# Expert results added to their tokens by TensorE instead of through a buffer in DRAM

## What is computed

```python
x = x + hierarchical_moe(rmsnorm(x, norm2_g), ...)
return rmsnorm(x, final_g)

def hierarchical_moe(h, ...):
    ...                                  # group, top 2 experts of it, their weights
    def expert_block(args):
        e, rows_tok, rows_w = args
        xb = tok[rows_tok]
        a = xb @ w_gate[e]               # 1024 x 512
        u = xb @ w_up[e]                 # 1024 x 512
        y = (jax.nn.silu(a) * u) @ w_down[e]     # 512 x 1024
        return (y * rows_w[:, None]).astype(tok.dtype)
    ...
    out = jnp.zeros((T, D), tok.dtype).at[row_tok].add(ys.reshape(n_rows, D))
```

## Time and profile before

| | |
|---|---|
| median of 3 runs | 1699.04 us (1697.4 to 1700.35) |
| the profiled execution, its time | 1699.08 us |
| the profiled execution, its span in the trace | 1697.2 us |
| TensorE busy | 1477.6 us (87%), in the last quarter less |
| VectorE, ScalarE, GpSimd busy | 34%, 28%, 29% |
| DMA engines, from 1200 us to 1594 us | busy all the time, 424 GB/s |
| indirect DMAs, issue to landing | gathers 14.1 us, scatters 10.4 us (median) |

### The profile page before, as it was taken

How to read it: one execution, slowest core, us unless ns; L and a number is a source line. 1 busy time by engine, 2 the same in 40 slices (tenths; PEclk the granted TensorE clock), 3 DMA queues, 4 the chain that set the end, 5 groups by cost and what they waited for, 6 DMA issues and landing times.

```text
span 1697.2 us, 18562 instructions
## 1 busy us (share of the span) xinstructions
PE 1477.6 (87%) x7132; PEld 979.0 (58%) x7133; DVE 585.2 (34%) x964; ACT 475.4 (28%) x818; POOL 487.8 (29%) x286
## 2 busy tenths in 40 slices
PE   7999999999699999999995999993977778787792
PEld 5975667887588888788684675573322233222230
DVE  3146654213633333321418695745100000000003
ACT  4245564222433333221424324221100000000001
POOL 3531134444334444444332373422001000010000
PEclk9999999999899999999997999996999998999996
DMA  7323002232223332223222221167899999999894
GB/s 287 109 88 86 1 2 63 90 97 88 86 87 99 99 100 91 96 89 97 87 87 88 81 75 52 48 245 293 327 428 427 426 429 427 425 423 422 358 384 192
DMA packets 48263, 317.33 MB, mean 187 GB/s; under 512 B 7696, under 2 KB 7696, under 8 KB 35776
## 3 DMA queue, kind: packets, MB, share of 16 engines
q1 hardware_dynamic: 40240, 295.13, 45.5%
q0 software_dynamic: 7376, 19.13, 3.1%
q10 hardware_dynamic: 576, 2.10, 0.3%
HBM read 308.00 MB, written 14.68 MB: 190 GB/s over the span
## 4 chain that ended last, share of the span: by engine, by line
PE 64%; DMA 19%; DVE 9%; issue 3%; ACT 2%; POOL 1%; SPq 0%; POOLq 0%; DVEq 0%; ACTq 0%
PE banks L357 24%; DMA arena<-experts 17%; PE banks L387 11%; PE banks L981 8%; PE banks L1961 3%; PE banks L868 2%; PE banks L367 2%; PE banks L1003 2%; PE banks L1890 2%; PE banks L1906 2%; DMA rows<-arena 1%; PE banks L725 1%; PE banks L1873 1%; PE banks L726 1%; PE banks L1877 1%
## 5 line engine op out<-in xcount | busy, mean ns | idle before, releaser
L335 POOL TENSOR_TENSOR arena_r<-ring,arena_r 128x1024 fp32r<-128x1024 f32 x143 | 354.0, 2477 | 503.5 <-ACT arena_r L320 503.5
L357 PE MATMUL banks<-hT_r,arena_r 128*128 128x512 f32 x1216 | 391.8, 392 | 8.5 <-DVE arena_r L1738 5.4
L320 ACT ACTIVATE arena_r<-ring 128x1024 fp32r<-128x1024 f32 x143 | 151.3, 1059 | 517.0 <-PE banks L357 318.2
L357 PE MATMUL banks<-arena_r 128*128 128x512 f32 x800 | 293.4, 392 | 0.0
L981 PE MATMUL banks<-ring,arena 128*64 128x512 f32 x720 | 228.1, 622 | 59.0 <-DMA arena<-experts 40.4
L357 PEld LDWEIGHTS banks<-hT_r,arena_r 128*128 128x128 f32 x1216 | 228.7, 188 | 67.0 <-issue 9.3
L387 PE MATMUL banks<-arena_r 128*128 128x512 f32 x784 | 187.5, 393 | 3.6 <-POOL arena_r L335 3.6
L981 PEld LDWEIGHTS banks<-ring,arena 128*64 128x64 f32 x720 | 75.0, 143 | 200.1 <-issue 149.0
L387 PEld LDWEIGHTS banks<-arena_r 128*128 128x128 f32 x784 | 147.2, 188 | 38.3 <-POOL arena_r L335 5.3
L357 PEld LDWEIGHTS banks<-arena_r 128*128 128x128 f32 x800 | 150.5, 188 | 32.3
L605 POOL DMA_INDIRECT back<-arena,at_out x16 | 16.1, 1007 | 430.9 <-DVE arena L1479 216.5
(11 more groups left out here) (421 smaller groups left out, 1812.3 us busy)
## 6 DMA issues: line engine op xcount, KB each, us to landing
arena<-experts SPq DMA_DIRECT2D x49, 2048.0 KB, 19.0
ring<-experts SPq DMA_DIRECT2D x45, 2048.0 KB, 18.3
ring<-stream SPq DMA_DIRECT2D x163, 512.0 KB, 3.5
rows<-arena POOLq DMA_DIRECT2D x8, 512.0 KB, 7.1
arena<-back SPq DMA_DIRECT2D x8, 512.0 KB, 7.1
grow<-grows POOLq DMA_DIRECT2D x5, 512.0 KB, 4.5
resid<-x ACTq DMA_DIRECT2D x4, 512.0 KB, 5.3
hT<-experts SPq DMA_DIRECT2D x1, 2048.0 KB, 19.1
```

Of the source, the lines that this page charges most:

```text
L320: nc.scalar.activation(parts(name, m)[:, 0, :], tile(tile_n), ACT.Copy).then_inc(S["w_high"], 1)
L335: nc.gpsimd.tensor_tensor(w[:, 1, :], tile(tile_n), plain(w[:, 0, :]), ALU.subtract).then_inc(S["w_low"], 1)
L357: last = nc.tensor.matmul(pb[:, bank, :], w[:, a, k * P:(k + 1) * P], b[:, k, :], start=(k == 0 and part == 0), stop=(k == ND - 1 and part ...
```

## The change

The store of `rows` is made once (four DMAs), and the index of a slot is the token. The buffers `back`, `G`, `ysb` and `xo` are gone, with the scatters and the loads of `back`.

In their place the router also makes `p_of`, the weight of each slot (eight more tensor_scalars of 128 x 128 and eight more matmuls), and keeps the token of each slot in f32 (`token_of`). For each pair VectorE forms `spread_r`, a 0/1 matrix of 128 slots x 512 tokens (one comparison). The down product of 128 slots x 1024 is taken out of PSUM times the slot's weight, in two parts whose sum is f32: ScalarE writes `y_high`, rounded to fp32r (twice 128 x 512), and VectorE `y_low`, the rest (twice 128 x 512, each behind the ScalarE part). `place` then multiplies: for each of four blocks of 128 tokens four matmuls of 128 x 512 in fp32r (two halves of the width, high and low), and VectorE adds the two banks to `X` (`add_pair`, 128 x 1024). `place` of pair b - 1 stands between the gate and the up product of pair b, and uses banks 3, 4 and 5, 6 in turn; the third and fourth block wait for the add that frees their banks. That of pair 15 stands behind it, with all eight banks.

`Xg` is cleared by GpSimd before each gather from pair 2 on. The three chunks loaded ahead are now chunk 0 of pair 4, chunk 1 of pair 8 and chunk 2 of pair 12; the third is issued when the first two gathers have landed. The pair loops are written out on all engines. The norm's squares on ScalarE wait for the last adds directly, the final scaling is made in place in `X`, and the branch to the overflow passes stands behind the last adds on VectorE. Unused constants are dropped.

```diff
-        rows = nc.dram_tensor("rows", (2 * T, D), F32).ap()
-        back = nc.dram_tensor("back", (2 * T, D), F32).ap()
+        at_tok, at_p = sb("at_tok", [P, 1]), sb("at_p", [P, 1])
+        rows = nc.dram_tensor("rows", (T, D), F32).ap()
...
-        ysb = ar3(24576, 2, D)
+        y_high, y_low = [ar_r(off, D) for off in (24576, 25600)]
...
+        token_of, p_of = ar(27136, P), colt[:, 512:512 + P]
+        spread_r = colt_r[:, 0:T]
+        token_row = cs("alibi")
+        STEADY, LAST = [(3, 4), (5, 6), (3, 4), (5, 6)], [(0, 1), (2, 3), (4, 5), (6, 7)]
...
-        SPARE = (N_PAIR - 2, [[(hT[:, :, :].rearrange("p k t -> p (k t)"), 0, CHUNK)], [(ar(0, CHUNK), 0, CHUNK)],
-                              [(ar(4096, 1536), 0, 1536), (ar(6656, 1536), 1536, 3072), (junk[:, :], 3072, CHUNK)]])
...
+        SPARE = {0: 4, 1: 8, 2: 12}
...
-            for j in range(2 * NT):
-                pool.dma_start(rows[j * P:(j + 1) * P, :], xn[:, j % NT, :]).then_inc(S["rows_st"], 16)
+            for i in range(NT):
+                pool.dma_start(rows[i * P:(i + 1) * P, :], xn[:, i, :]).then_inc(S["rows_st"], 16)
...
+            def cleared(b, q):
+                pool.wait_ge(S["x_tr"], b * 2 + 2)
+                pool.sem_inc(S["gathers"], 1)
+                nc.gpsimd.memset(Xg[:, q, :], 0.0).then_inc(S["xg_zero"], 1)
+                pool.wait_ge(S["xg_zero"], b)
+            for b in range(N_PAIR):
+                if b >= 2:
+                    cleared(b, b % 2)
+                gather(b, b % 2, idx[:, BLOCKS * b:BLOCKS * b + 1])
...
+                    sp.dma_start(place, EX[6 * SPARE[c] + c, :, first:end]).then_inc(S["spare_in"], 16)
             sp.wait_ge(S["w_used"], W_EXP)
             spare_in(0)
-            sp.wait_ge(S["rows_st"], 16 * 2 * NT)
+            sp.wait_ge(S["rows_st"], 16 * NT)
             spare_in(1)
             sp.wait_ge(S["counts_out"], 1)
+            sp.wait_ge(S["xg_in0"], 16)
+            sp.wait_ge(S["xg_in1"], 16)
             spare_in(2)
-            with sp.Fori(1, SPARE[0]) as b:
+            for b in range(1, N_PAIR):
                 for c in range(6):
-                    sp.wait_ge(done[c // 2], b)
-                    sp.dma_start(chunk(c), EX[b * 6 + c, :, :]).then_inc(chunk_in[c], 16)
-            for b in range(SPARE[0], N_PAIR):
-                for c in range(3 if b == SPARE[0] else 0, 6):
-                    sp.wait_ge(done[c // 2], b - 1 if c < 3 and b > SPARE[0] else b)
-                    sp.dma_start(chunk(c), EX[b * 6 + c, :, :]).then_inc(chunk_in[c], 16)
+                    if not spared(b, c):
+                        sp.wait_ge(done[c // 2], b - 1 if spared(b - 1, c) else b)
+                        sp.dma_start(chunk(c), EX[b * 6 + c, :, :]).then_inc(chunk_in[c], 16)
...
-            sp.wait_ge(S["fin_go"], 1)
-            for i in range(NT):
-                for c in range(2):
-                    sp.dma_start(G[:, 2 * i + c, :], back[(NT * c + i) * P:(NT * c + i + 1) * P, :]).then_inc(S[f"back{i}"], 16)
             for i in range(NT):
                 sp.wait_ge(S["fin_y"], i + 1)
-                sp.dma_start(out[i * P:(i + 1) * P, :], xo[:, i, :]).then_inc(S["out_st"], 16)
+                sp.dma_start(out[i * P:(i + 1) * P, :], X[:, i, :]).then_inc(S["out_st"], 16)
...
+            for j in range(2 * NT):
+                pe.wait_ge(S["slot_ready"], 2 * NT + j + 1)
+                last = nc.tensor.matmul(pb[:, 2, 0:P], slot_row[:, j, :], slot_value[:, j, :], start=(j == 0), stop=(j == 2 * NT - 1))
+            last.then_inc(S["rank_mm"], 1)
...
+                if not isinstance(b, int) or b >= 1:
+                    pe.wait_ge(S["y_lo"], b * 2)
+                    pe.wait_ge(S["added"], b * NT if not isinstance(b, int) else b * NT - 1)
+                both_in(b, 4)
...
+            def place(b, banks):
+                pe.wait_ge(S["spread"], b + 1)
+                pe.wait_ge(S["y_hi"], b * 2 + 2)
+                pe.wait_ge(S["y_lo"], b * 2 + 2)
+                for i in range(NT):
+                    if banks is STEADY and not (isinstance(b, int) and b == 0 and i < 2):
+                        pe.wait_ge(S["added"], b * NT + max(i - 1, 0))
+                    elif banks is LAST and i == 0:
+                        pe.wait_ge(S["added"], b * NT)
+                    for h in range(2):
+                        for part, y in enumerate((y_high, y_low)):
+                            last = nc.tensor.matmul(pb[:, banks[i][h], :], spread_r[:, i * P:(i + 1) * P], y[:, h * 512:(h + 1) * 512],
+                                                    start=(part == 0), stop=(part == 1))
+                    last.then_inc(S["placed"], 1)
+            def pair_pe(b, half, q):
                 turn_rows(b, half, q)
                 pe.wait_ge(S["x_ev_dve"], b + 2)
                 pe.wait_ge(S["x_ev_act"], b + 2)
-                product(b, 0, 0, S["ex_gate"], skipped)
-                product(b, 2, 1, S["ex_up"], skipped)
+                product(b, 0, 0, S["ex_gate"])
+                if isinstance(b, int) and b >= 1:
+                    place(b - 1, STEADY)
+                product(b, 2, 1, S["ex_up"])
                 turn_hidden(b)
-                down(b, skipped)
+                down(b)
             pe.wait_ge(S["counts_out"], 1)
-            with pe.Fori(0, SPARE[0] // 2) as turn:
-                for q in range(2):
-                    pair_pe(turn * 2 + q, turn, q)
-            for q in range(2):
-                pair_pe(SPARE[0] + q, SPARE[0] // 2, q, q > 0)
+            for b in range(N_PAIR):
+                pair_pe(b, b // 2, b % 2)
+            place(N_PAIR - 1, LAST)
...
-            for q in range(2):
-                pair_act(q, 0, q)
-            with act.Fori(1, N_PAIR // 2) as turn:
-                for q in range(2):
-                    pair_act(turn * 2 + q, turn, q)
+                for h in range(2):
+                    nc.scalar.activation(y_high[:, h * 512:(h + 1) * 512], pb[:, 3 + h, :], ACT.Copy, scale=p).then_inc(S["y_hi"], 1)
+            act.wait_ge(S["p_ready"], 1)
+            for b in range(N_PAIR):
+                pair_act(b, p_of[:, BLOCKS * b:BLOCKS * b + 1])
+            for i in range(NT):
+                act.wait_ge(S["added"], NT * (N_PAIR - 1) + i + 1)
+                square(act, "n5", i, X[:, i, :])
+                root(act, "n5", i)
...
+            for j in range(2 * NT):
+                TS(slot_value[:, j, :], cs("iota"), column[:, j:j + 1], RT[:, 880 + j:881 + j], ALU.is_equal, ALU.mult)\
+                    .then_inc(S["slot_ready"], 1)
+            for i in range(NT):
+                L(TS(token_row[:, i * P:(i + 1) * P], cs("iota"), float(P * i), None, ALU.add))
             counts = RT[0:1, 1400:1432]
             nc.vector.tensor_copy(counts, pb[0:1, 0, 0:32]).then_inc(S["counts_out"], 1)
-            def pair_rows(b, half, q):
+            dve.wait_ge(S["rank_mm"], 3)
+            nc.vector.tensor_copy(p_of, pb[:, 2, 0:P]).then_inc(S["p_ready"], 1)
...
+            def spread_rows(tokens):
+                TS(spread_r, token_row, tokens, None, ALU.is_equal).then_inc(S["spread"], 1)
+            def pair_hidden(b, p):
                 dve.wait_ge(S["ex_up"], b + 1)
                 dve.wait_ge(S["ex_sig"], b + 1)
                 TT(hb, sil, pb[:, 1, :], ALU.mult).then_inc(S["ex_hid"], 1)
-                dve.wait_ge(S["ex_down"], b + 1)
-                if not opening(b):
-                    dve.wait_ge(S[f"y_st{q}"], half * 16)
-                nc.vector.tensor_copy(ysb[:, q, 512:1024], pb[:, 4, :]).then_inc(S["y_ev_dve"], 1)
-            pair_rows(0, 0, 0)
+                for h in range(2):
+                    dve.wait_ge(S["y_hi"], b * 2 + h + 1)
+                    STT(out=y_low[:, h * 512:(h + 1) * 512], in0=pb[:, 3 + h, :], scalar=p, in1=plain(y_high[:, h * 512:(h + 1) * 512]),
+                        op0=ALU.mult, op1=ALU.subtract).then_inc(S["y_lo"], 1)
+            def add_pair(b, banks):
+                for i in range(NT):
+                    dve.wait_ge(S["placed"], b * NT + i + 1)
+                    if not (isinstance(b, int) and b == 0):
+                        dve.wait_ge(S["added"], b * NT + i - (NT - 1))
+                    first, second = banks[i]
+                    TT(X[:, i, :], X[:, i, :], pb[:, first:second + 1, :].rearrange("p b c -> p (b c)"), ALU.add).then_inc(S["added"], 1)
...
+            for b in range(N_PAIR):
+                if b:
+                    pair_rows(b)
+                    add_pair(b - 1, STEADY)
+                spread_rows(token_of[:, BLOCKS * b:BLOCKS * b + 1])
+                pair_hidden(b, p_of[:, BLOCKS * b:BLOCKS * b + 1])
+                if b == 0:
+                    dve.wait_ge(S["over_ready"], 1)
+                    some = dve.value_load(over[0:1, 0:1], min_val=0, max_val=1)
+            add_pair(N_PAIR - 1, LAST)
...
-            for i in range(NT):
-                dve.wait_ge(S[f"back{i}"], 32)
```

(6 more changed lines are left out.)

163 lines of the change are left out of this document (64 added, 99 removed).

## The result

The changed kernel takes 1703.82 us (median of 8 runs, 1702.47 to 1710.01), the kernel before, beside it, 1699.01 (8 runs, 1696.73 to 1700.35). The ratio is 1.0035, with a 95% interval of 1.0023 to 1.0047: **slower** by 4.8 us, or 0.35%. The profiled execution took 1703.4 us, with a span of 1701.5, against 1697.2 before.

| stretch | before | after | difference | forecast |
|---|---|---|---|---|
| to the first add behind the last dense product (L1363, now L1360) | 1137.36 | 1148.94 | +11.6 | 0 |
| from there to the eviction of pair 0 | 79.0 | 68.9 | -10.1 | -7.5 |
| eviction of pair 0 to that of pair 15 | 451.1 | 465.85 | +14.7 | +11.9 |
| eviction of pair 15 to the end | 29.7 | 17.8 | -12.0 | -12.0 |

The account below looks back on a forecast made before the run. Loads bound the expert part before; the change was to move the bound to TensorE's chain. Span 1697.2 + 10.9 + 1.0 - 7.5 - 12.0 = 1689.6, with 1.88 us around it 1691.5 us; range 1676 to 1705.

Parts of the forecast that it names:

- The one nearest in time, at 1704.5: Rival: the start gives nothing and place takes 5.2 us; 1704.5 us, chance 0.09.
- The loads to TensorE: Expert pairs: the bound moves from the loads, 29.3 us a pair, to TensorE; DMA share 0.95 to 0.98.
- The chain: TensorE's work per expert pair: 25.0 + 4.6 + 1.2 = 30.8 us; +10.9 us over fifteen pairs.
- The eviction: Between pairs: the gate product starts 2.94 us after the eviction's start instead of 1.62; 1.2 us more a pair.
- The register load: VectorE's load of a register ahead of pair 1: 1.0 us more (0 to 2).
- The clock: Rival: longer waits in the pairs make TensorE's granted clock fall, 1.7 us each; ten falls give 1708.5 us; chance 0.17.
- The start: Before pair 0: half the stores and one chunk less ahead let the first gather land earlier; -7.5 us.
- The third chunk's hold: In the start: holding this chunk until both gathers are in leaves 2.1 MB less ahead of the gather, 5 us.
- The tail: From the last eviction to the end: 17.7 us instead of 29.7, -12.0 us.
- the branch behind them: In the tail: VectorE's branch behind the last add takes 1.0 us (0 to 2.5).

Follow-up runs that it names:

- e1: Changed kernel with the old list of constants, so the arena stands at its old address: 1691.49 us, ratio 0.9964 to the kernel before.
- e2: Kernel before with the changed kernel's list of constants and nothing else of the change: 1711.84 us, ratio 1.0075.
- x1: On e1, VectorE copies the turned rows before making the low parts, and the gate product waits for ScalarE's copy only at its fifth step: 1665.92 us.
- e9: On e1, place multiplies only the high parts, 8 matmuls a pair instead of 16: 1677.72 us.
- e14: On e1, the third early chunk is issued once the counts are out, without waiting for the first two gathers: 1691.43 us.
- e10: On e1, the tokens are stored in DRAM twice, as before the change (eight stores): 1702.96 us.
- e3: Changed kernel with an empty 64-byte buffer between the constants and what follows, arena 128 bytes off a multiple of 256 from hT: 1698.4 us.
- e6: On e1, an empty 64-byte buffer at the very start moves every buffer by 64 bytes and keeps all distances: 1692.67 us.
- x2: On x1, TensorE also turns the next pair's rows behind the up product, while VectorE makes the hidden product: 1660.28 us, ratio 0.9774.
- x3: On x2, the dense down product's rows stand 32 columns lower, at a multiple of 256 bytes from the weights: 1658.21 us.

## Why the prediction was wrong

The value, 1691.5, lay 12.3 us under the measured one, inside the range. The direction, faster with a chance of 0.68, was wrong.

**The step that failed** is one that the sum does not even show as a term: it starts from the old span, 1697.2, and adds only what happens behind the router, taking what stands ahead of it as it was. The term for the stages ahead of the router was put at nothing without a reason. The change speaks against that in one place, the shorter `CSTS` ("unused constants are dropped"), which shifts the arena by 448 bytes. In the up stage it changed the pitch of the fp32r matmuls from 226.2 to 233.9 ns, which is 7.3 us between 492 and 705 us, and with other stages it came to 11.6 us by the last dense product. e1 and e2 show that this list by itself is worth 12.3 and 13.0 us, in either kernel. With it the prediction's own terms give 1703.1, and the changed kernel takes 1703.8.

None of the rivals was this. The one nearest in time, at 1704.5, was made of other things: a start that is 4 us later than forecast (one that gives nothing, as it is called, would be 7.5 later), where it came 2.6 us sooner, and place at 5.2 us, where it took 4.8. That the value lies inside the range is luck: the range was not made for this term.

**The loads to TensorE.** Right. The DMA share fell to 0.96, between the 0.95 and 0.98 that were named, and the waits for loads are gone.

**The chain.** Forecast 30.8 us a pair, measured 30.93 (29.8 to 31.5 were allowed). Place takes from the gate's last matmul to the up's first 1325.43 - 1320.66 = 4.8 us, forecast 4.6, and the adds hold it as described: the third group starts 2.50 us after the first, forecast 2.39.

```profile
1320.66 2.11 PE L996 MATMUL banks<-arena_r,colt_r 128*128 128x512 f32 x8
...
1323.16 2.34 PE L996 MATMUL banks<-arena_r,colt_r 128*128 128x512 f32 x8 [0.39 <-DVE resid L1495]
```

The eviction, too: ScalarE starts at 1310.86, and the gate product at 1313.64, 2.78 us later, forecast 2.94.

```profile
1313.64 0.64 PE L956 MATMUL banks<-hT,arena 128*64 128x512 f32 x1 [1.81 <-DVE arena L1473]
```

The size was right, but the prediction took this wait as the price of the change. x1 shows that most of it was the price of one order: the two low parts are not needed until place, 7 us later, and stood ahead of the copy on which TensorE waits. (x1 also lets the gate product start without ScalarE's copy; the two edits were not run apart.)

**The register load**, 1.0 us ahead of pair 1: the first pair is 31.12 us against 30.93, so 0.2.

**The clock.** The rival with a chance of 0.17 happened in small. One pair of the changed kernel took 32.61 us at a granted clock of 0.95, in the gate product behind the ordinary wait of 1.8 us, which took 8.8 us there instead of 7.0. e1 had two such pairs, e9 four, the other runs with this wait one to three, and x1, whose wait is 0.35 us, none. The row of that product on the timeline:

```profile
1530.17 8.78 PE L956 MATMUL banks<-ring,arena 128*64 128x512 f32 x32 [1.80 <-DVE arena L1473]
```

A fall costs 1.7 us, as the prediction took from the earlier trace rows; ten falls were far too many. The Trainium skill (TensorE: Matmul & The Clock Gate, A second HAM failure mode: psum-queue depth-cycling) would have them come from short waits between groups of matmuls; in the changed kernel the fall stands behind the long wait after the transposes, not behind the short ones inside place, and x1, which keeps the short ones and shortens the long one, has none. The falls may also explain part of the spread of the changed kernel's eight runs, though only one of them was profiled: the slowest, 1710.01 us, has the lowest mean clock (0.971) and the fastest, 1702.47, the highest (0.976).

**The start.** Forecast -7.5, measured -10.6 in e1 (1216.35 to 1205.70) and -10.1 in the changed kernel. The time of the row transposes was right: 1179.99 us in e1, forecast 1181. The way there was not. The stores were not done at 1172 but before 1162.45, when the chunk that waits for them was issued; the four stores, issued from 1154.34 on, were done within 8.1 us, where eight took 20.4 from the last one's issue. So the index alone set the gather. The third chunk's hold, to which 5 us were put down, gains nothing (e14). And 2.3 us came from TensorE, which no longer idles for 9 us (e10; 14 in the kernel before) and is at the full clock sooner; the sum had no term for that.

**The tail.** Forecast 17.7 us, measured 17.8. The first add ends 4.8 us behind the eviction's start, forecast 4.6. All four are done after 9.2 us, forecast 8.1, since the second and the third wait for their matmuls; but the branch behind them, forecast at 1.0, costs nothing, and so the scalings start where they should. VectorE's adds and its last scaling:

```profile
1687.34 1.22 DVE L1495 TENSOR_TENSOR resid<-resid,banks 128x1024 f32<-128x1024 f32 x1 [1.49 <-PE banks L996]
...
1690.42 2.48 DVE L1495 TENSOR_TENSOR resid<-resid,banks 128x1024 f32<-128x1024 f32 x2 [0.49 <-PE banks L996]
...
1697.19 1.28 DVE L1559 SCALAR_TENSOR_TENSOR resid<-resid,st,grow 128x1024 f32<-128x1024 f32 x1
```

Together the terms behind the router gave -7.6 in the forecast. Without the shift, e1 against before, the profiled spans differ by -6.1 (1691.1 - 1697.2) and the medians by -7.4. That is partly luck: in e1 the start gained 3.1 us more than forecast, and the fifteen pairs, 467.4 us, cost 4.4 more (3.3 for two clock falls, 1.9 for the 0.13 in each pair, less 0.8 for the register).

## What to carry to other kernels

A diff that changes the size of anything in SBUF changes the distances between all operands on its two sides, and with them the speed of code it does not touch; before costing the edit itself, list what moves, and keep the distances with an empty buffer. Compare two profiles from the start of the span and not from the edit on: an offset that grows evenly in a stretch where nobody waits is a change in the pitch of an instruction. And when a change adds work to an engine that becomes the bound, look at the order in which its helpers serve it: here two instructions moved behind a copy, and one wait put off, were worth 25.6 us, against 7.4 for the whole change without its shift of addresses. Whether a distance that is good for one stage is good for the next has to be looked up in the profile: e3's shift made the merge product faster and the up stage slower.

## What the runs showed of the hardware

- fp32r matmuls of 128x128 by 128x512, issued back to back with full clock, have a pitch that depends on the distance in SBUF between their operands. In the up stage it is 226.2 ns a matmul at a multiple of 256 bytes, 228.6 at 128 off, 232.8 at 192 off and 233.9 at 64 off, and moving both buffers by 64 bytes costs nothing (e6). In two other stages a multiple of 256 was the fastest too, but 128 off cost 6.7 ns (merge product, before against e3) and 5.8 ns (down product, x2 against x3). The Trainium skill (SBUF — State Buffer, SBUF: two separate sides) has TensorE never wait for anyone at its own SBUF ports, and says that only the port pair of VectorE and GpSimd causes contention between engines; here it stayed at full clock without a wait for an engine and yet its pitch grew by up to 3.4% with where its own operands stood. The down product, whose operands are all in the arena, kept its pace when the arena moved: ScalarE's rows of the two kernels are 9.6 us apart at 714 us and still at 829. It went from 231.5 to 225.7 ns when its rows were put at a multiple of 256 (x3).
- The same sensitivity was not seen in the experts' f32 matmuls: their pair distance is 30.93 us with the arena at either distance.
- A transfer that waits for the same semaphore as another can be its worst neighbour: with four stores less the second early chunk ran 16 us earlier and was nearly through when the gather was issued, which then took 4.6 us to its use instead of 8.5 (e1 and e10; the chunk alone was not moved).
- TensorE's granted clock fell from its upper level (2.4 GHz) in 1 of 15 pairs in the changed kernel, 2 in e1, 4 in e9 and none in x1. The wait ahead of the gate product is 1.8 us in the first three and 0.35 in x1. In the pair looked at closest, 1.00 stood until the wait, 0.50 from 1531 to 1534 us in the gate product, and 1.00 again behind it. The same wait left the clock at 1.00 in most pairs, so it does not decide a fall by itself. x3 has one fall, behind a wait of 2.9 us for a load.
